# Two tables loaded once instead of once per group, and the memory map that makes room for them

## The reference

```
h += W_o( headnorm( concat[ MLA(xn), ShortGatedConv(xn) ] ) )      xn = RMSNorm(h)
h += CrossAttn(RMSNorm(h), RMSNorm(mem))                           4 heads, 256 memory tokens
h += PEER(RMSNorm(h))
out = RMSNorm(h)
```

```
q = hn @ w_pq                      8 heads x 2 halves x 64
s = q . sub_keys                   128 scores for each head and half
s_top, i_top = top_k(s, 16)        in both halves; 16 x 16 sums; the best 16 of them
experts = i_top[0] * 128 + i_top[1]          16 experts per head, 128 per token
out = sum over the 128 experts e of  gelu(hn . u_e) * gate_e * v_e
```

## Time and profile before

| | |
|---|---|
| time, median of 3 runs | 3315.94 us (3306.09 to 3317.48) |
| the profiled execution | 3298.2 us, span 3296.4 us |
| busy: PE, DVE, ACT, POOL | 79%, 69%, 41%, 37% of the span |
| DMA | 1242.16 MB, mean 377 GB/s over the span |
| issued by POOL (expert rows) | 1024 gathers, 1073.81 MB, 78.9% of the time of 16 DMA engines |

### The profile page before, as it was taken

The page is one execution under the profiler, slowest core; times in us unless marked ns, Lnnn a source line. Parts: engine busy times, 40 slices in busy tenths (PEclk is TensorE's granted clock), DMA queues, the critical chain, the costliest instruction groups (busy, mean ns, idle before and its releaser), DMA issues.

```text
span 3296.4 us, 28771 instructions
## 1 busy us (share of the span) xinstructions
PE 2612.6 (79%) x7912; PEld 1412.5 (43%) x7912; DVE 2287.6 (69%) x4808; ACT 1353.1 (41%) x3634; POOL 1224.0 (37%) x1051
## 2 busy tenths in 40 slices
PE   8988889867987898787877788787888666666676
PEld 7665556444335464453334454463335222222222
DVE  2021377797676867887776867786787877777765
ACT  1122243476443444673433334673533333333333
POOL 0000143344344443344444433334444444444443
PEclk9999899989998999898988999898989898888888
DMA  6433399999999999999999999999999999999998
GB/s 245 166 147 139 128 355 416 388 378 391 423 423 390 426 427 423 366 416 414 418 421 425 420 405 403 346 379 407 413 427 418 427 424 427 428 422 409 427 427 343
DMA packets 186033, 1242.16 MB, mean 377 GB/s; under 512 B 21904, under 2 KB 31120, under 8 KB 39952
## 3 DMA queue, kind: packets, MB, share of 16 engines
q0 software_dynamic: 147456, 1073.81, 78.9%
q1 hardware_dynamic: 36112, 153.93, 11.9%
q10 hardware_dynamic: 2304, 12.58, 0.9%
HBM read 1223.73 MB, written 16.52 MB: 376 GB/s over the span
## 4 chain that ended last, share of the span: by engine, by line
DMA 38%; PE 33%; DVE 13%; ACT 6%; issue 5%; POOL 3%; DVEq 2%; ACTq 0%; SPq 0%; POOLq 0%
DMA rows<-in_experts,idx 33%; PE ps L1029 11%; PE ps L1062 8%; PE ps L1048 5%; DVE rows L1491 4%; DVE acc_v L1502 4%; POOL rows L680 3%; DMA wbuf<-in_w_conv 3%; PE ps L1087 2%; ACT L840 1%; PE ps L1100 1%; PE ps L1105 1%; ACT probs L840 1%; DVE gsq L1658 1%; ACT probT L851 1%
## 5 line engine op out<-in xcount | busy, mean ns | idle before, releaser
L680 POOL DMA_INDIRECT rows<-in_experts,idx x1024 | 1220.3, 1192 | 2048.1 <-PE ps L1029 960.9
L1029 PE MATMUL ps<-rows,diag 128*128 128x512 f32 x2712 | 1442.4, 671 | 425.6 <-ACT diag L733 398.6
L1491 DVE CUSTOM_DVE_ANT_0 rows<-rows,hn 128x1024 f32<-128x1024 f32 x1024 | 1237.2, 1224 | 553.9 <-DMA rows<-in_experts,idx 536.5
L1029 PEld LDWEIGHTS ps<-rows,diag 128*128 128x128 f32 x2712 | 550.7, 213 | 1151.9 <-ACT diag L733 605.8
L722 ACT ACTIVATE gelu<-dots 128x1 f32<-128x1 f32 x1024 | 206.7, 202 | 1396.4 <-DVE dots L1491 1380.6
L1502 DVE SCALAR_TENSOR_TENSOR acc_v<-rows,weight,acc_v 128x1024 f32<-128x1024 f32 x346 | 444.0, 1283 | 0.6 <-ACT weight L726 0.6
L1062 PE MATMUL ps<-T,wbuf 128*128 128x256 f32 x1536 | 375.6, 395 | 71.7 <-DMA wbuf<-in_w_conv 34.3
L1062 PEld LDWEIGHTS ps<-T,wbuf 128*128 128x128 f32 x1536 | 300.6, 198 | 172.1 <-issue 58.4
L1048 PE MATMUL ps<-wbuf,T 128*128 128x512 f32 x640 | 316.4, 632 | 38.4 <-ACT T L884 16.9
L726 ACT ACTIVATE weight<-gelu,gate 128x1 f32<-128x1 f32 x1024 | 301.8, 295 | 75.2 <-issue 3.1
L733 ACT ACTIVATE diag<-ident,weight 128x128 f32<-128x128 f32 x678 | 272.3, 402 | 57.1 <-issue 1.3
(11 more groups left out here) (205 smaller groups left out, 1901.6 us busy)
## 6 DMA issues: line engine op xcount, KB each, us to landing
wbuf<-in_w_conv SPq DMA_DIRECT2D x24, 1024.0 KB, 9.1
wbuf<-in_w_o SPq DMA_DIRECT2D x16, 1024.0 KB, 9.0
wbuf<-in_w_pq SPq DMA_DIRECT2D x16, 1024.0 KB, 8.9
rows<-in_experts,idx POOLq DMA_INDIRECT x1024, 12.6
wbuf<-cross_a SPq DMA_DIRECT2D x12, 1024.0 KB, 12.2
wbuf<-cross_b SPq DMA_DIRECT2D x12, 1024.0 KB, 11.3
wbuf<-in_w_cq SPq DMA_DIRECT2D x8, 768.0 KB, 9.4
wbuf<-in_w_ckvr SPq DMA_DIRECT2D x8, 576.0 KB, 8.3
```

Of the source, the lines that this page charges most:

```text
L680: pool.indirect_dma_start(out=rows[n % RR][:], out_offset=None, in_=w["experts"][:, :], in_offset=bass.IndirectOffsetOnAxis(ap=idx[:, b % ...
L1029: mm = pe.matmul(ps[:, 6 + half, :], diag[:, m % DIAGS, :], rows[n % RR][:, D + half * HALFC:D + (half + 1) * HALFC], start=(k == 0), stop ...
L1491: dve.tensor_tensor_reduce(out=rows[n % RR][:, 0:D], in0=rows[n % RR][:, 0:D], in1=hn[:, b % 3, :], scale=1.0, scalar=0.0, op0=ALU.mult, o ...
```

## The change

**g_ffn** and the sub-keys (`pkeys`) get 4 KB each behind the last row buffer. SP loads them once, behind the loads of the weight folding and ahead of group 0. The loads in each group go, and with the one of g_ffn a wait on SP (`filled(sp, g, "oT", HB - 1)`). The score matmuls read `pkeys`. The chunk of the keys leaves the ring, so a group has 32 chunks instead of 33, and each chunk behind that place follows another one in its slot.

The room comes from four edits. `rest` goes: DVE strikes out the best eight in the scores themselves (`match_replace` in place). `junk` goes out of the resident part: squares are written to a dead part of `hn` (`hn_junk`), to a place inside `xprobs` (`junk`) or, at the start, to a place ahead of the rows (`first_junk`). `krs` moves into a shared stretch. `cand_v` and `cand_r`, which had shared `rest`, get 864 bytes each of their own.

```diff
-            + [(w["w_pq"], c, WCHUNK) for c in range(2)]
-            + [(w["keys"], 0, PHEADS * PKEYS)]
-            + [(w["w_pq"], c, WCHUNK) for c in range(2, 4)])
+            + [(w["w_pq"], c, WCHUNK) for c in range(4)])
-CHUNKS = 33
+CHUNKS = 32
...
-        last += [JOB[g, "pq", 1] if g else JOB[g, "pqb", 1]] * 2 + [JOB[g, "ps", 4 * HB - 1]] + [JOB[g, "pq", 3]] * 2
+        last += [JOB[g, "pq", 1] if g else JOB[g, "pqb", 1]] * 2 + [JOB[g, "pq", 3]] * 2
...
-        krs = own("krs", [P, HB, ROPE])
-        junk = own("junk", [P, D], BF16)
+        hn_junk = [at(f"hn_junk{s}", where[0] + 4 * s, [P, D], BF16) for s in range(3)]
         hn = own("hn", [P, 3, D])
-        rest = own("rest", [P, 8, PKEYS])
-        cand_v = at("cand_v", where[0] - 4, [P, HHALF, CAND])
-        cand_r = at("cand_r", where[0] - 2, [P, HHALF, CAND])
+        cand_v = own("cand_v", [P, HHALF, CAND])
+        cand_r = own("cand_r", [P, HHALF, CAND])
...
+        krs = at("krs", s0 + 27, [P, HB, ROPE])
-        g_ffn = at("g_ffn_b", s0 + 20, [P, D])
+        junk = at("junk", s0 + 16, [P, D], BF16)
         r0 = s0 + 36
         rows = [at(f"rows{s}", r0 + 8 * s, [P, 2 * D]) for s in range(RR)]
+        g_ffn = at("g_ffn_b", r0 + 8 * RR, [P, D])
+        pkeys = at("pkeys", r0 + 8 * RR + 4, [P, PHEADS * PKEYS])
...
-                filled(sp, g, "oT", HB - 1)
-                sp.dma_start(g_ffn[:], w["g_ffn"].to_broadcast([P, D])).then_inc(gffn_in, 16)
...
+            sp.dma_start(g_ffn[:], w["g_ffn"].to_broadcast([P, D])).then_inc(gffn_in, 16)
+            sp.dma_start(pkeys[:], w["keys"][0]).then_inc(pkeys_in, 16)
             for g in range(NG):
                 front(g)
...
-                    features(g, "pq", i, [(C_PQ + 3 * (i // 2), (2 * i + m) % 4 * P, HALFC) for m in range(2)],
+                    features(g, "pq", i, [(C_PQ + 2 * (i // 2), (2 * i + m) % 4 * P, HALFC) for m in range(2)],
-                    keys = chunk(chunk_no(g, C_KEYS))
-                    chunk_in(pe, chunk_no(g, C_KEYS))
+                    pe.wait_ge(pkeys_in, 16)
-                        dve.match_replace(rest[:, n, :], best_v[:, n, 0:8], scores(c, hd), LOWEST)
+                        dve.match_replace(scores(c, hd), best_v[:, n, 0:8], scores(c, hd), LOWEST)
-                    dve.wait_ge(gffn_in, 16 * (g + 1))
+                    dve.wait_ge(gffn_in, 16)
```

More of the change, by code:

```diff
@@ L127, in block_chunks @@
             + [(w["cross_b"], c, WCHUNK) for c in range(4)]
-            + [(w["w_pq"], c, WCHUNK) for c in range(2)]
-            + [(w["keys"], 0, PHEADS * PKEYS)]
-            + [(w["w_pq"], c, WCHUNK) for c in range(2, 4)])
-C_CQ, C_CKVR, C_CONV, C_UQ, C_UKV, C_HEAD, C_O, C_A, C_B, C_PQ, C_KEYS = 0, 2, 4, 10, 12, 13, 16, 20, 24, 28, 30
-CHUNKS = 33
+            + [(w["w_pq"], c, WCHUNK) for c in range(4)])
+C_CQ, C_CKVR, C_CONV, C_UQ, C_UKV, C_HEAD, C_O, C_A, C_B, C_PQ = 0, 2, 4, 10, 12, 13, 16, 20, 24, 28
+CHUNKS = 32
 HRING = 4
@@ L350, in layer_kernel @@
         scores_s = own("scores_s", [P, HB, 2 * PHEADS, PKEYS])
-        rest = own("rest", [P, 8, PKEYS])
-        cand_v = at("cand_v", where[0] - 4, [P, HHALF, CAND])
-        cand_r = at("cand_r", where[0] - 2, [P, HHALF, CAND])
-        start_f = at("start_f", where[0] - 4, [P, HHALF, TOPK])
-        sel_f = at("sel_f", where[0] - 3, [P, 2, EXPERTS // 2])
+        start_f = at("start_f", where[0], [P, HHALF, TOPK])
+        cand_v = own("cand_v", [P, HHALF, CAND])
+        sel_f = at("sel_f", where[0], [P, 2, EXPERTS // 2])
+        cand_r = own("cand_r", [P, HHALF, CAND])
         top_v = own("top_v", [P, HHALF, TOPK])
@@ L393, in layer_kernel @@
         sq = at("sq", s0 + 28, [P, LT, GT])
-        g_ffn = at("g_ffn_b", s0 + 20, [P, D])
+        junk = at("junk", s0 + 16, [P, D], BF16)
         r0 = s0 + 36
         rows = [at(f"rows{s}", r0 + 8 * s, [P, 2 * D]) for s in range(RR)]
+        g_ffn = at("g_ffn_b", r0 + 8 * RR, [P, D])
+        pkeys = at("pkeys", r0 + 8 * RR + 4, [P, PHEADS * PKEYS])
+        first_junk = at("first_junk", s0 + 34, [P, D], BF16)
         mems = at("mems", s0, [P, 2, D])
@@ L421, in layer_kernel @@
         gffn_in = sem("gffn_in")
+        pkeys_in = sem("pkeys_in")
         mem_in = sem("mem_in")
@@ L711, in row_work @@
                         act.drain()
-                        act.activation(junk[:], acc_v[:, (b - 1) % 2, :], ACT.Square, accum_out=fss[:, (b - 1) % 2:(b - 1) % 2 + 1])
+                        act.activation(hn_junk[(b - 1) % 3][:], acc_v[:, (b - 1) % 2, :], ACT.Square, accum_out=fss[:, (b - 1) % 2:(b - 1) % 2 + 1])
                         act.drain()
@@ L766, in enter @@
                     act.drain()
-                    act.activation(junk[:], (xs if g else h)[:, b, :], ACT.Square, accum_out=ss[:, b:b + 1])
+                    act.activation((junk if g else first_junk)[:], (xs if g else h)[:, b, :], ACT.Square, accum_out=ss[:, b:b + 1])
                 act.drain()
@@ L987, in _ @@
                 act.drain()
-                act.activation(junk[:], memx[:, m, :], ACT.Square, accum_out=ss[:, 12 + m:13 + m])
+                act.activation(first_junk[:], memx[:, m, :], ACT.Square, accum_out=ss[:, 12 + m:13 + m])
             act.drain()
@@ L1297, in scores @@
                                            T2[c * PDIM:(c + 1) * PDIM, hd, tokens(b)],
-                                           keys[c * PDIM:(c + 1) * PDIM, hd * PKEYS:(hd + 1) * PKEYS], start=True, stop=True)
+                                           pkeys[c * PDIM:(c + 1) * PDIM, hd * PKEYS:(hd + 1) * PKEYS], start=True, stop=True)
                             if hd % 4 == 3:
@@ L1389, in topk @@
                     for c, hd in some:
-                        dve.max(best_v[:, c * heads + hd, 8:16], rest[:, c * heads + hd, :])
+                        dve.max(best_v[:, c * heads + hd, 8:16], scores(c, hd))
                     dve.drain()
@@ L1393, in topk @@
                         n = c * heads + hd
-                        dve.max_index(best_i[:, n, 8:16], best_v[:, n, 8:16], rest[:, n, :])
+                        dve.max_index(best_i[:, n, 8:16], best_v[:, n, 8:16], scores(c, hd))
                     yield
```

## The result

The changed kernel takes 3325.03 us (median of 12 runs, 3316.79 to 3335.44), the kernel before 3314.20 us (12 runs). The ratio is 1.0039, 95% interval 1.0025 to 1.0054: slower by about 13 us (8 to 18; the medians lie 10.8 us apart), where 13.5 us less had been forecast. At 0.4% the difference is small, but with 12 runs of each kernel it is clear of the noise. The profiled execution took 3318.55 us, its span is 3316.7 us.

What follows compares the result with a forecast made beforehand. From slice six on, 86% of the span, the kernel was taken as bound by DMA bytes at about 426 GB/s. Savings of 7.4 + 2.5 + 0.9 + 2.7 = 13.5 us from 3315.9 gave 3302 us, range 3284 to 3322.

Steps and rivals of the forecast that it cites:

- The edits without a price: Moved squares and `krs`, in-place striking out, and score and norm waits for landed transfers: taken as costing nothing.
- rival C: Row buffers start 192 bytes past a 256-byte multiple, so gathers take 1/32 more: 81 us, time 3383; chance 0.17.
- The bytes: Bound part, groups 1 to 3: six fewer loads of g_ffn and keys, 3.15 MB at 426 GB/s, 7.4 us saved.
- The start of the row work: End of group 0: third w_pq chunk issued almost 100 us earlier, so row work starts 2.5 us sooner; bounds 0 and 3.1.
- The next group's first chunk: w_cq issued after group 0's block queries, its 0.786 MB carried between 402 and 440 us: 0.9 us saved, bounds 0 and 1.8.
- The dip of group 1: DMA falls to 192 GB/s from 1048 to 1053 us; with the third w_pq chunk there already, 2.7 us saved.
- the chunks' waits: Shorter waits of the late w_pq chunks and the next w_cq: 6.1 us in the sum (2.5 + 0.9 + 2.7).
- rival A: All PE waits for w_pq paid in full, 13.3 us instead of 5.2; 23 us saved, time 3293; chance 0.20.
- In place: Striking out in the scores, 128 instructions of 276 ns on DVE: taken as nothing, perhaps 3 us if each took twice as long.

Runs made afterwards that it cites:

- the kernel that only loads: No layer: SP only loads the expert table into SBUF in 15 phases of differing piece size and offset; one execution, 1906.25 us.
- the hole: Changed kernel on boundaries, keys loaded once but their ring place kept empty, so late w_pq chunks and next w_cq wait as before: 3306.90 us, 0.9989 of the kernel before.
- on boundaries: Changed kernel with weight ring and row buffers put back on multiples of 256 bytes: 3299.97 us, ratio 0.9960 to the kernel before.

## Why the prediction was wrong

**The step that failed** is "The edits without a price": the sum has no term for what the new memory map does to the gathers. The squares and `krs` "go to other addresses with the same instructions" was read for the engines only. The memory map moved under the DMA engines too, and the row buffers went off a multiple of 256 bytes. That costs 26 us in this kernel, against 13 us saved. The prediction's own sign of rival C, a rate in pure row work under 424 GB/s, is what came: 420. The ratio does lie within 0.5% of no change, which had 0.54 of the chance, but by luck: 13 us saved and 26 lost happen to leave little.

**Rival C** named the cause, rows off a multiple of 256 bytes, and had 0.17 of the chance. Its price was three times too high, 81 us and not 26. Per packet it took 1/32, 9.6 ns on 306, as if a cut cost as much as the 256 bytes it carries; measured are 4.7 ns, 1.5%, half of that. By its packets that would be 8192 row packets per engine x 4.7 ns = 38 us; 22 to 31 us were measured in the kernels with the rows off. The share of the gathers' queue times the span says where the rest is: it is 2626 to 2634 us in the four layer kernels with the rows off and 2598 to 2606 us in the seven with them on a boundary, 29 us more. So a gather's packet pays some 3.5 ns over the whole kernel (29 us / 8192, an estimate), where in pure row work it pays 4.4 (8192 x 16 / 420 less 8192 x 16 / 426), as in the kernel that only loads. Outside the full stretches it pays less; why is open. With 26 us in the place of 81 the prediction's own rival would have read 3315.9 + 26 - 13.5 = 3328; with 81 it lay so far off that the range left it out and ended at 3322, below the 3325 measured. No row read before the change prices it; a price between nothing and 81 us should have been in the range as an unknown cost.

**The bytes**: 3.15 MB, right. Their price was confirmed by adding bytes (13.9 us for 5.41 MB), not by taking them away: without 3.15 MB and with the old waits (the hole) 3.6 us were measured, from 1 us longer to 8 shorter, an interval that just holds the sum's 7.4.

**The start of the row work**: 2.5 us forecast, 3.2 us between the two traces (10.3 to 7.1 us from the scores to the first row product). The order of events is as told: PE works 8 instructions on the third chunk and then waits for the fourth, 0.96 us ("under 1 us", 0.65 by its working). One thing is missing in the prediction: it took the 20 query matmuls at 6.19 us in both kernels. They took 1.99 + 2.86 = 4.85 us in the new one, with a granted clock of 1.00 (2.4 GHz) all the time; before, the clock was 0.50 (1.2 GHz) in their first 3 us and 0.72 in the mean (before twice, then after):

```profile
407.00:408.50 1.50, 1.50 (x4) 1.23 (x5) 1.12 (x4) 1.48 (x2) 0.00 (x0) 0.50 0.90 382
406.75:412.70 5.95, 5.95 (x20) 5.01 (x21) 5.21 (x24) 3.61 (x10) 0.00 (x0) 0.72 0.28 117
399.95:405.70 5.75, 4.79 (x22) 3.60 (x20) 1.99 (x9) 5.50 (x9) 0.00 (x0) 1.00 0.70 295
```

PE had idled 3.10 us ahead of them in the one and idled 0.96 us between them in the other. That the shorter idle time kept the clock up fits this, but was not tried.

And 2.5 us was read from one execution, the one with the shortest wait. The same stretch on boundaries, with the hole and then in the changed kernel:

```profile
408.17 1.16 PE L1303 MATMUL ps<-pkeys,T 64*128 64x128 f32 x16 [0.77 <-ACT T L924]
413.06 7.39 PE L1070 MATMUL ps<-T,wbuf 128*128 128x256 f32 x20 [3.73 <-DMA wbuf<-in_w_pq]
420.29 3.60 PE L1037 MATMUL ps<-rows,diag 128*128 128x512 f32 x8
```

```profile
401.16 1.16 PE L1299 MATMUL ps<-pkeys,T 64*128 64x128 f32 x16 [0.77 <-ACT T L920]
408.28 3.70 PE L1033 MATMUL ps<-rows,diag 128*128 128x512 f32 x8 [0.17 <-ACT diag L737]
```

From the scores to the first row product it is 12.1 us against 7.1, 5.0 us less. In the nine layer kernels with the old waits this stretch takes 10.3 to 13.4 us, and the 10.3 of the trace before is the least of them; in the two with the new waits it is 7.1. (When the scores themselves begin, 399 to 408 us, differs from trace to trace and also between kernels that do the same until then, so only the stretch is compared.)

**The next group's first chunk** goes out right behind the fourth w_pq chunk. The timeline of SP, after, against the earlier trace rows:

```profile
398.09 0.33 SPq L562 DMA_DIRECT2D wbuf<-in_w_pq  x1
398.46 27.91 SPq L562 DMA_DIRECT2D wbuf<-in_w_cq  x2
```

Its issue moved forward by 40 us, as told. Its 0.9 us were not measured apart.

**The dip of group 1** is gone, 1.01 and 419 GB/s from 1048 to 1053 us. In most of the other kernels with the old waits it comes some 10 us later, so that this window alone does not show it. On boundaries, with the hole and then in the changed kernel:

```profile
1060.00:1070.00 10.00, 10.00 (x31) 6.55 (x30) 6.62 (x9) 2.12 (x8) 4.36 (x4) 0.80 0.67 250
1060.00:1070.00 10.00, 5.99 (x37) 4.67 (x38) 4.90 (x7) 4.60 (x11) 1.88 (x2) 0.66 1.02 425
```

That is 10 x (1 - 250/427) = 4.1 us, where the sum had 2.7. With 5.0 us for the start, the two account for most of the 9.6 us of the chunks' waits, as far as one trace of each kernel can tell, without rival A: its waits in groups 2 and 3 are not needed, and no run tried them apart.

**In place**: striking out in the scores takes 276 ns as before:

```profile
L1388 DVE MATCH_REPLACE8 scores_s<-best_v,scores_s 128x128 f32<-128x128 f32 x128 | 35.4, 276 | 0.0
```

## What to carry to other kernels

When a change takes tiles away or adds some, work out the new start of every tile behind them; for tiles that are written by a stream of DMA packets that bounds the kernel, keep it on a multiple of 256 bytes, even at the cost of padding. Read the rate in a quiet, full stretch before and after: a share of 1.01 in both with fewer GB/s means that the packets themselves have become dearer, as here 426 and 420, whatever else the change did. A wait that becomes a term of the sum wants more than one trace: the 3.10 us read here were the least of nine. And an edit "only to make room" is part of the change and gets a line of its own in the sum.

## What was not expected of the hardware

A packet into SBUF that starts off a multiple of 256 bytes costs 4.2 to 4.7 ns more on its DMA engine in the kernel that only loads, at 1, 2, 4 and 8 KB with an offset of 192 bytes and at 8 KB for 32, 64 and 128 too. An offset of 192 bytes on the read side, in HBM, cost nothing at 4 KB. Packets on a boundary have a fixed part of the same size: 306 ns at 8 KB and 1024 x 16 / 386 = 42.4 ns at 1 KB give 37.7 ns per KB and 4.7 ns besides, an estimate from two of the phases; 2 and 4 KB fit it (80.1 and 155.7 ns measured, 80.1 and 155.5 by it).
